# Token-by-feature projection of q, k and v, and another order of score pairs, in a hybrid decoder layer on one core

## The reference

```python
h = rmsnorm(x, norm1); proj = h @ w_in
qa = apply_rope(rmsnorm(qa.reshape(B, S, 12, 128), qn_a), cos, sin) * 128 ** -0.5
ka = apply_rope(rmsnorm(ka.reshape(B, S, 4, 128), kn_a), cos, sin)
va = va.reshape(B, S, 4, 128)
# 3 query groups per kv head: (window, dilation) = (128,1), (512,4), (2048,16)
# query t sees keys t - j*dilation, j = 0..window/dilation; softmax per group,
# the three group outputs combined weighted by their softmax denominators
oa = dilated_attention(qa, ka, va)
y = sigmoid(ga) * (oa @ w_proj_a) + sigmoid(gb) * (ob @ w_proj_b); x = x + y @ w_out
x = x + (silu(h2 @ w_ffn_gate) * (h2 @ w_ffn_up)) @ w_ffn_down
```

## Time and profile before

| | before |
|---|---|
| median of 3 runs | 1899.29 us (1898.77 to 1900.63) |
| the profiled execution, its own time | 1900.71 us |
| its span | 1899.2 us |
| PE busy | 1814.6 us, 96% of the span |
| PEld busy | 1520.1 us, 80% |
| DVE busy | 1130.0 us, 59% |
| ACT busy | 714.9 us, 38% |
| POOL busy | 548.9 us, 29% |
| granted TensorE clock, mean | 0.992 |

### The profile page before, as it was taken

The page is one execution under the profiler, slowest core; times in us unless marked ns, Lnnn a source line. Parts: engine busy times, 40 slices in busy tenths (PEclk is TensorE's granted clock), DMA queues, the critical chain, the costliest instruction groups (busy, mean ns, idle before and its releaser), DMA issues. The chain is left out here.

```text
span 1899.2 us, 27059 instructions
## 1 busy us (share of the span) xinstructions
PE 1814.6 (96%) x8932; PEld 1520.1 (80%) x8932; DVE 1130.0 (59%) x1960; ACT 714.9 (38%) x1430; POOL 548.9 (29%) x654
## 2 busy tenths in 40 slices
PE   5999999999999799999997999999999999999999
PEld 4888878878877788889885788877888888888887
DVE  6552752752753866757586554587555555665776
ACT  5342342343243325353536222354233323334443
POOL 2211221221322605141422000006556555620120
PEclk9999999999999999999999999999999999999999
DMA  5111222212211111111024423224232323178764
GB/s 150 45 56 57 67 67 67 63 60 68 67 55 57 67 36 35 55 33 55 17 83 165 148 75 115 86 88 133 89 110 84 128 92 109 63 251 315 266 210 172
DMA packets 155027, 187.99 MB, mean 99 GB/s; under 512 B 9168, under 2 KB 105712, under 8 KB 154432
## 3 DMA queue, kind: packets, MB, share of 16 engines
q1 hardware_dynamic: 142352, 150.30, 24.5%
q0 software_dynamic: 7984, 28.29, 4.5%
q10 hardware_dynamic: 4608, 8.39, 1.1%
HBM read 144.59 MB, written 42.35 MB: 98 GB/s over the span
## 5 line engine op out<-in xcount | busy, mean ns | idle before, releaser
L2132 PE MATMUL bank<-act_hi,w_hi 128*128 128x512 f32 x952 | 382.5, 402 | 2.9 <-DVE act_lo L1766 2.5
L2134 PE MATMUL bank<-act_hi,w_lo 128*128 128x512 f32 x952 | 372.4, 391 | 0.0
L2133 PE MATMUL bank<-act_lo,w_hi 128*128 128x512 f32 x952 | 371.6, 390 | 0.0
L2132 PE MATMUL bank<-ca,wq 128*128 128x512 f32 x528 | 206.9, 392 | 6.4 <-DVE wq L1877 3.9
L2132 PEld LDWEIGHTS bank<-act_hi,w_hi 128*128 128x128 f32 x952 | 179.6, 189 | 41.1 <-DVE act_lo L1766 4.2
L2134 PEld LDWEIGHTS bank<-act_hi,w_lo 128*128 128x128 f32 x952 | 179.2, 188 | 38.5
L2133 PEld LDWEIGHTS bank<-act_lo,w_hi 128*128 128x128 f32 x952 | 179.7, 189 | 34.8
L2134 PE MATMUL bank<-ca,wq 128*128 128x512 f32 x528 | 206.3, 391 | 0.0
L2133 PE MATMUL bank<-ca,wq 128*128 128x512 f32 x528 | 206.2, 390 | 0.0
L1448 DVE TENSOR_TENSOR w_lo<-w_raw,w_hi 128x1024 fp32r<-128x1024 f32 x80 | 98.3, 1236 | 66.8 <-ACT w_hi L937 66.8
L2132 PEld LDWEIGHTS bank<-ca,wq 128*128 128x128 f32 x528 | 99.6, 189 | 29.3 <-issue 3.4
(11 more groups left out here) (356 smaller groups left out, 3853.9 us busy)
## 6 DMA issues: line engine op xcount, KB each, us to landing
w_raw<-in_w_in SPq DMA_DIRECT2D x60, 512.0 KB, 3.8
rawd<-in_w_ffn_down SPq DMA_DIRECT2D x99, 256.0 KB, 5.0
rx<-y_scratch SPq DMA_DIRECT2D x77, 256.0 KB, 4.3
wr<-in_w_ffn_gate SPq DMA_DIRECT2D x11, 1024.0 KB, 5.3
wr<-in_w_ffn_up SPq DMA_DIRECT2D x11, 1024.0 KB, 5.4
y_scratch<-sq SPq DMA_DIRECT2D x11, 1024.0 KB, 4.3
y_scratch<-yq SPq DMA_DIRECT2D x33, 256.0 KB, 2.0
gate_scratch<-gbuf ACTq DMA_DIRECT2D x32, 256.0 KB, 2.1
```

The costliest lines, as they stand in the source:

```text
L2132: pe.matmul(ps, lhs_hi, rhs_hi, start=first, stop=False, skip_group_check=onto)
L2133: pe.matmul(ps, lhs_hi, rhs_lo, start=False, stop=False, skip_group_check=onto)
L2134: return pe.matmul(ps, lhs_lo, rhs_hi, start=False, stop=last, skip_group_check=onto)
```

## The change

- **v once, at the start.** v of all four heads is projected before the first head, 8 calls of a new `four`: the activations are the stationary operand, the weights (`w_hi`, `w_lo`) the moving one, and the result is token by feature. ACT copies each result and writes it to a new DRAM tensor `v_scratch` (`v_out`). SP then reads `vt` of a head with three strided DMAs (`load_vt`). The `v` jobs are gone.
- **k and q by `four`.** A head's k, q0, q1, q2 take 8 calls: four with two token tiles and two heads' blocks (`n` = 2, 48 matmuls of 256 columns), four with one tile and all four blocks (24 of 512 columns). The `a` jobs, `qk_raw` and the DVE sum are gone: ACT squares each 128x128 block from PSUM with an accumulated sum, four instructions a call.
- **16 steps a head** in place of 18; rotated results are transposed two steps behind their projection.
- **Pairs in another order.** `UNITS` names the two blocks of a pair, `UNITS_AT` the step behind which it is taken: pair 0 after step 3, the others from step 6 on.
- **Merging of the head before** at other places: `merge_diffs` within step 1, `merge_norm` after step 3, `mul` 0 within step 5, `mul` 1 and 2 in step 8, ahead of pair 3; `merge_weights` on POOL after the fourth rotation.
- **Four weight slots**, shared memory laid out anew; x half by half at the start; `ab_raw` loaded last.
- **Stage B's first head:** POOL does `d2` ahead of `S0`.

The core of the diff:

```diff
-    TA, TB, TC = 9, 6, 6
+    TV, TA, TB, TC = 4, 8, 6, 6
...
+    QK = [((0, 1), 0, 2), ((0, 1), 2, 2), ((2,), 0, 4), ((3,), 0, 4), ((4,), 0, 4), ((5,), 0, 4),
+          ((6, 7), 0, 2), ((6, 7), 2, 2)]
+    UNITS = [(0, 1), (2, 3), (8, 10), (12, 14), (4, 5), (6, 7), (9, 11), (13, 15), (16, 17), (18, 19), (20, 21), (22, 23)]
+    UNITS_AT = {3: [0], 6: [1], 7: [2], 8: [3, 4], 9: [5], 10: [6], 11: [7, 8], 12: [9], 13: [10, 11], 14: [12, 13], 15: [14]}
+    HI_A = {6: [4], 7: [5], 8: [6], 10: [7], 11: [8], 12: [9]}
+        return banks[0 if s == 15 else (5, 0, 1)[s % 3]]
...
             merge_stats(h - 1)
+            for j in range(4):
+                pool_rope(h, j)
             merge_weights(h - 1)
-            for j in range(8):
+            for j in range(4, 8):
                 pool_rope(h, j)
             merge_sum(h - 1)
...
-                work = ["d0", "W0", "d1", "S0", "d2", "d3"] + last
+                work = ["d0", "W0", "d1", "d2", "S0", "d3"] + last
...
+            for s in range(16):
+                act.wait_ge(st_ready, base + s + 1)
+                if s < 8:
+                    act.wait_ge(t2_ready, 8 * h + (s - 1 if s >= 2 else 0))
+                    for i in range(4):
+                        act.activation(rot[:, s % 2, i, :], bank_a(s)[:, P * i:P * i + P], ACT.Square,
+                                       accum_out=qk_st[:, 0, s, i:i + 1]).then_inc(t1_sq, 1)
...
+                for k in HI_A.get(s, []):
+                    hi_a(k % 4, 2 * h + k // 4 + 2)
...
+            def qk_norm(j):
+                n = 8 * h + j
+                tiles, c0, size = QK[j]
+                dve.wait_ge(t1_sq, 4 * n + 4)
+                dve.tensor_scalar(qk_st[:, 1, j, :], qk_st[:, 0, j, :], 1.0 / P, EPS,
+                                  ALU.mult, ALU.add).then_inc(t1_var, 1)
+                for k in HI_A.get(j, []):
+                    lo_a(A0 + TA * h + k, k % 4)
+                if behind and j == 1:
                     merge_diffs(h - 1)
...
+                if behind and j == 5:
+                    merge_mul(h - 1, 0)
+                dve.wait_ge(t1_rstd, n + 1)
...
+            lo_a(A0 + TA * h + 2, 2)
+            lo_a(A0 + TA * h + 3, 3)
+            for s in range(16):
+                if s < 8:
+                    qk_norm(s)
+                    rope(s)
+                    if behind and s == 3:
+                        merge_norm(h - 1)
+                else:
+                    for k in HI_A.get(s, []):
+                        lo_a(A0 + TA * h + k, k % 4)
+                    if behind and s == 8:
+                        merge_mul(h - 1, 1)
+                        merge_mul(h - 1, 2)
+                for j in UNITS_AT.get(s, []):
+                    dve_unit(j)
...
+        def four(ps, j):
+
+            tiles, c0, n = QK[j]
+            for i, tt in enumerate(tiles):
+                o = ps[:, P * n * i:P * n * i + P * n].rearrange("p (c d) -> p c d", d=P)
+                toks = slice(P * tt, P * tt + P)
+                for kt in range(NK):
+                    cols = slice(P * kt, P * kt + P)
+                    mm = three(o, act_hi[:, kt, toks], act_lo[:, kt, toks],
+                               w_hi[:, c0:c0 + n, cols], w_lo[:, c0:c0 + n, cols], kt == 0, kt == NK - 1)
+            return mm
...
+        for g in range(8):
+            turn_x(g)
+        for j in range(8):
+            if j < 2:
+                pe.wait_ge(lo_done, 2 * j + 2)
+                pe.wait_ge(nt_lo, 8)
+            if j >= 3:
+                pe.wait_ge(st_evac, j - 2)
+            four(banks[j % 3], j).then_inc(st_ready, 1)
+            if j in (1, 2):
+                for g in range(4 * j + 4, 4 * j + 8):
+                    turn_x(g)
+            if j == 3:
+                pe.wait_ge(ab_lo_done, 1)
+                pe.wait_ge(nt_lo, 16)
...
+            for s in range(16):
...
+                elif s < 11:
+                    pe.wait_ge(t1_gain, 4 * (8 * h + s - 3) + 4)
...
+                if s < 8:
+                    four(bank_a(s), s).then_inc(st_ready, 1)
+                else:
+                    stream(bank_a(s), s // 2 - 4, act_hi, act_lo, s % 2, slot=s // 2 - 4).then_inc(st_ready, 1)
+                if 2 <= s < 10:
+                    j = s - 2
+                    pe.wait_ge(t2_evac, 8 * h + j)
+                    pe.wait_ge(rot_done, 16 * h + 2 * j + 2)
+                    for i in range(4):
+                        mm = pe.transpose(banks[6][:, P * i:P * i + P], rot[:, j % 2, i, :], ident[:, :])
+                    mm.then_inc(t2_ready, 1)
+                for j in UNITS_AT.get(s, []):
+                    if j < NB:
+                        pe_s(j)
+                    if 2 <= j < NB + 2:
+                        pe_t(j - 2)
+                    if j >= 3:
+                        pe_pv(j - 3)
```

More of the change, by code:

```diff
@@ L116, in decoder_layer @@
     mhalf = small[:, 48:56]
[L117 to L167, removed]
     with ExitStack() as mem:
@@ L267, in decoder_layer @@
     phase_end = sem("phase_end")
-    raw_in = [sem(f"raw_in{i}") for i in range(3)]
+    raw_in = [sem(f"raw_in{i}") for i in range(4)]
     hi_done, lo_done = sem("hi_done"), sem("lo_done")
@@ new lines, in _ @@
+        act.preload_act_table_set("natural_log_exp_and_others")
+        for tt in range(4):
+            square(tt)
+        hi_a(0, 1)
+        hi_a(1, 1)
+        act.wait_ge(gain_in, 16)
+        for g in range(8):
+            norm_hi(g)
+        hi_a(2, 1)
+        hi_a(3, 1)
+        for tt in range(4, 8):
+            square(tt)
+        act.wait_ge(ab_in, 16)
+        act.copy(ab_w[:, :, 0:LR], ab_raw[:, :, :]).then_inc(ab_hi_done, 1)
+        v_out(0)
+        v_out(1)
+        for g in range(8, 12):
+            norm_hi(g)
@@ L967, in _ @@
+        v_out(2)
+        for g in range(12, 16):
+            norm_hi(g)
+        v_out(3)
+        act.wait_ge(ab_ready, 2)
+        act.copy(ab_t[:, 0:HALF], banks[3][0:2 * LR, :]).then_inc(ab_done, 1)
+        act.copy(ab_t[:, HALF:S], banks[4][0:2 * LR, :]).then_inc(ab_done, 1)
+        v_out(4)
+        v_out(5)
         act.wait_ge(pos_step, 9)
@@ L971, in _ @@
         act.preload_act_table_set("natural_log_exp_and_others")
[L972 to L974 removed]
         leave_phase(act)
+        v_out(6)
+        hi_a(0, 2)
+        hi_a(1, 2)
+        v_out(7)
         enter_phase(act, 1)
@@ new lines, in _ @@
+        for j in range(8):
[11 more added lines that the diff above has]
+                pe.wait_ge(nt_lo, 16)
+                for xh in range(2):
+                    t = slice(HALF * xh, HALF * xh + HALF)
+                    for kt in range(NK):
+                        pe.matmul(banks[3 + xh][0:2 * LR, :], ab_w[:, kt, :], act_hi[:, kt, t], start=(kt == 0),
+                                  stop=False)
+                        mm = pe.matmul(banks[3 + xh][0:2 * LR, :], ab_w[:, kt, :], act_lo[:, kt, t], start=False,
+                                       stop=(kt == NK - 1))
+                    mm.then_inc(ab_ready, 1)
+            if j == 4:
+                pe.wait_ge(ab_ready, 2)
+                pe.sem_inc(phase_end, 1)
```

562 lines of the change are left out of this document (287 added, 275 removed), and 3 rows, old and new, of the table JOBS_A.

## The result

The changed kernel takes 1914.40 us (median of 4 runs, 1912.58 to 1916.74) against 1899.08 before: ratio 1.0082, 95% interval 1.0068 to 1.0096. It is slower by 15.3 us; the forecast was 1897.6, and the range ended at 1907.

A forecast was written before the change was run, and what follows sets the result against it. PE, busy 96%, was taken as the bound. Stage A: 78.7 + 470.8 + 46.5 + 8.4 = 604.4 us for 598.4, 6.0 lost; B's first stream 0.2 later, B gains 7.9: net 1.7 faster, median 1897.6, range 1884 to 1907.

The forecast's parts named there:

- Start: Before head 0: v calls begin at 22.2 us, head 0 at 78.7, a gain of 3.7; clock fall of 2.1 counted apart.
- Head 0: First head, with no merge: 117.7 us without waits plus 6.6 of new waits.
- Without waits: A head with no waits of PE: 117.7 us in place of 141.1, four times 470.8.
- rival (d): Matmul forms: `four` at 256 columns costs as much as at 512, 53 us more, 1950; chance 0.02.
- Step 8: Later heads: PE waits for pair 2's maximum, pair 1's copy and pair 0's output copy, 10.5 us a head.
- rival (b): `nmax` of pair 3 is held by POOL's sum, 2.1 us a head in three heads, 1904; chance 0.22.
- my own case: The main forecast, 1897.6 us, spanning 1892 to 1903; chance 0.38.
- Steps 11 and 14: Late in a head: new waits of 1.3 us.
- step 6: Later heads: bank 6 is freed late, since ACT sits in exp of pair 0 behind `merge_norm`; 0.9 us.
- The clock: PE falls to half clock at the start and behind step 8 in three heads: four falls at 2.1, 8.4 us.
- Stage B: First head: `d2` ahead of `S0` removes PE's 7.9 us wait and the half clock later; gain 7.9, bounds 0 and 11.
- Rival (c): Stage B: moving `d2` brings nothing, since `dve_f` 1, now beside POOL, takes all; 1905, chance 0.08.
- (a): Rival: DVE and POOL don't queue for the small power, and the clock stays up; 1885, chance 0.30.

The follow-up runs named there:

- spread order: The changed kernel with one pair less in step 8: pair 3 in step 8, 4 in step 9, 5 and 6 in step 10; 1893.61 us.
- late read: The changed kernel with SP's read of v for the next head held until the statistics of the head before are read back; 1906.56 us.
- call 0 first: The changed kernel with POOL's power and product of call 0 ahead of the statistics' reads, and the merge's differences and exponentials one step later; 1907.38 us.
- reads on SP: The changed kernel with the eight reads of the statistics issued by SP in place of POOL, ahead of the read of v; 1903.56 us.
- late read and the spread order: The kernel of spread order and moved products, with the late read added; 1862.84 us.
- spread order and moved products: The spread order plus `mul` 1 and 2 behind the masks of pairs 3 and 4, and POOL's sum held until pair 6's maximum; 1872.55 us.

## Why the prediction was wrong

Point by point, against the profiled execution (forecast span 1897.5, measured 1911.1: 13.6 apart). The points below add up to it: -2.7 - 0.6 + 16.5 + 1.5, less 1.1 of gap ahead of stage B, which the last head's window holds and the forecast counted apart.

- **Start: 2.7 better, by luck of the execution.** Head 0 begins at 78.06, forecast 78.7, and the fall of the clock expected there, 2.1, did not come in it: PEclk is 1.00 in the whole window. But the variants above have the same start, and in 13 of these 16 profiled executions (the changed kernel's among the 16) the clock had fallen by the window from 24 to 26 us, and head 0 began at 79.1 to 79.8, against 77.4 to 78.1 in the other three. The term was right in kind and near in size. From the spread order's trace:

```profile
24.00:26.00 2.00, 2.00 (x12) 2.00 (x11) 1.29 (x2) 1.91 (x4) 0.00 (x0) 0.50 1.09 282
```

  The v calls' weights were in time; PE began them at 22.24, forecast 22.2 (whose splits, eight at 0.7, are 5.6 and not 5.8).
- **Head 0: 0.6 better, by two errors that cancel.** 123.7 us; forecast 117.7 + 6.6 = 124.3. The waits are 4.6 for 6.6, and PE's clock fell behind them (0.50 from 142 to 144), some 1.5 us, where the forecast had nothing. The 117.7 itself is right: with the spread order, at full clock, PE was busy 117.63 us in head 0.
- **The later heads: 16.5 worse, which is more than the whole error.** Forecast 117.7 + 13.3 + 2.1 = 133.1 for each; head 1 measured 118.7 + 16.4 + 4.0 = 139.1. By terms:
  - Without waits 118.7 for 117.7: one us undersized. The matmul forms cost what I took (no rival (d)). The forecast took 6.0 + 1.6 of waits out of 141.1, but the earlier trace rows have 6.1 in all, 141.1 - 135.0: of the 6.0 us between the first head and the second, 1.5 stand in PE's busy time.
  - Step 8: 10.7 us of waits, forecast 10.5 (1.7, 2.9 and 6.05 for 2.5, 3.0 and 5.0). That the sum fits is luck. POOL's power took 1.92 us beside DVE's product in one of three steps and 1.01 in the others, not 2 in each, and the first wait is shorter; and 1.8 of the third wait is the held maximum, which I had put into rival (b) and not into my own case. Without it the sum would be 8.9.
  - Steps 11 and 14: 1.3, as forecast. ACT's squares took 1.1 us a call, the two products 3.7 for 3.9.
  - **The step that failed: what stands before step 8.** I put 0.9 us on step 6 (and 0.6 on small gaps); the trace has 4.4 in head 1, 13.4 in the three. The place was named rightly (bank 6, with ACT in the exponential of pair 0); what makes its wait long was not. I priced the hold of call 4's power behind `merge_weights`, and put the hold of call 0's power behind `merge_stats` at nothing: before, POOL had finished that work 16 us ahead of the first variance, and the change took away the v streams that stood over it. I counted SP's queue too, but took "hidden" from the gate tiles alone, while `load_vt`, issued as POOL writes the statistics, and the tiles behind it drew out the wait for the small write from 1.98 us to 5.84 (the late read takes 2.5 of these 3.9 us back in head 1, and all in heads 2 and 3). The runs with the late read, with call 0 first and with the reads on SP give back 7.8, 7.0 and 10.8 us: this lag is worth about 3.6 us a head, and more if the reads on SP still leave some of it. The 1.9 us a head that stay even then are open.
  - **The clock, 4.0 a head for 2.1.** PE ran at 0.50 not only behind step 8 (some 2.6 us lost) but behind the unforeseen wait of 3.3 too (some 1.4 lost).
- **Stage B: 6.4 gained, forecast 7.9.** The wait named is gone. I had the slowing of `dve_f` 1 at 2.8 and nobody waiting for it; PE did, and its wait of 3.95 grew to 7.4. Rival (c) falls: `d2` alone brought 6.4.
- **The rivals.** (b) names a true mechanism; at 2.1 us a head, for 1.8 measured, its 1904 was still 10 too low, since it was laid on the same sum. Of (a) one half holds, that POOL's power is mostly not queued; the other, that the clock stays up, doesn't: behind the long waits it fell. No rival had its mechanism at the head of a head, so the range could not reach 1914. It took in the bounds of the costs that I had listed, and the missing one was not listed.

Read by what PE does, the forecast of the work that the change takes from a head was right (15.8 us; measured 135.0 - 118.7 = 16.3 at full clock), and so was the place where most of it goes again. With the waits of step 8 and about half of those before it removed, the changed kernel runs at 1862.8 us, 36.8 below the kernel before, and some 30 below the kernel before with stage B's edit.

## What to carry to other kernels

When a change removes work from the bound engine, list what stood under that work on the other queues, from the first instruction behind it: here two streams of 5.4 us had covered a DMA round trip and eight issues on POOL, and nothing in the profile before showed them as a wait of PE. A step in which three engines hand one item around needs a unit of the bound engine's work between its uses: one pair a step instead of two, by two changed numbers, was worth 20.8 us. And work that nobody waits for soon (the merge's products) goes behind the small instructions on its engine that somebody does wait for.

## What the runs showed of the hardware

- A DVE `tensor_scalar` of two elements a partition, from SBUF to SBUF, took 1.99 us in place of 0.17 beside POOL's 128x1024 sum: it began 0.4 us after the sum and ended with it. In all 48 cases it took 0.17 once the sum was held back. Its size doesn't protect it. The Trainium skill ("SBUF — State Buffer", section Who interferes with whom) says that this form can take the shared ports; the trace agrees.
- A write of 24 KB took 5.7, 5.5 and 5.3 us from issue to landing in the three heads when in head 1 it was issued 1.6 us after the first of three reads of 512 KB on another engine's queue; 3.1, 1.7 and 1.7 with these reads and the weight tiles behind them held back; and 1.7 to 1.8 in the kernel before. The DMA rows of head 1 (KB each, median us from issue to landing), the changed kernel and the late read of v, then the last line of the view of the write's line over the kernel before:

```profile
stat_scratch<-stat_sb POOLq DMA_DIRECT2D x1, 24.0 KB, 5.7
...
stat_scratch<-stat_sb POOLq DMA_DIRECT2D x1, 24.0 KB, 3.1
...
DMA to landing us min/median/max: 1.7/1.7/1.8
```

- Behind a wait of 3.3 us the granted clock fell to 1.2 GHz for a stretch, within two us after PE had taken up work again; behind the 2.1 us at the same place with the late read and the spread order it stayed at 2.4. The length of the wait alone doesn't tell which: with call 0 first on POOL the clock fell behind a wait of 2.27 us that ends at 241.3, and with the spread order and moved products it stayed at 1.00 behind one of 2.54 that ends at 218.7. Windows of the changed kernel about the wait that ends at 242.0, then of call 0 first, then of the late read with the spread order about its wait, which ends at 236.7:

```profile
240.00:242.00 2.00, 0.00 (x0) 0.00 (x0) 0.17 (x1) 1.88 (x11) 0.11 (x1) 1.00 0.04 6
242.00:244.00 2.00, 1.99 (x15) 1.99 (x16) 0.17 (x1) 1.30 (x9) 1.64 (x2) 0.86 0.49 98
244.00:246.00 2.00, 2.00 (x11) 2.00 (x10) 1.97 (x6) 0.33 (x1) 0.88 (x1) 0.50 0.86 307
...
243.00:245.00 2.00, 2.00 (x12) 2.00 (x11) 1.92 (x6) 0.64 (x3) 0.66 (x1) 0.50 0.90 313
...
236.00:238.00 2.00, 1.32 (x11) 1.32 (x12) 0.17 (x1) 1.18 (x7) 1.29 (x2) 1.00 0.00 0
238.00:240.00 2.00, 2.00 (x19) 2.00 (x18) 1.48 (x5) 1.00 (x6) 0.58 (x2) 1.00 1.08 332
```
